# Where the value products of two attention stages stand in TensorE's queue, and how independent matmuls are dealt out between them

## The reference

```python
for window, dil in DILATED_PATTERNS:      # (128, 1), (512, 4), (2048, 16)
    o, lse = band_attention(by_residue(q), by_residue(k), by_residue(v), window // dil)
    ...
w = jax.nn.softmax(jnp.stack(lses, axis=0), axis=0)
o = jnp.sum(w[..., None] * jnp.stack(outs, axis=0), axis=0)
```

```python
g = jax.nn.sigmoid(gates)...
o = g[..., 0:1] * o_cmp + g[..., 1:2] * o_s + g[..., 2:3] * o_w
```

## Time and profile before

| | us |
|---|---|
| median of 3 runs | 3198.38 (3194.66 to 3199.76) |
| the profiled execution, its own time | 3204.74 |
| its span | 3203.0 |
| TensorE busy | 3175.9 (99%) |
| VectorE, ScalarE, GpSimd busy | 1728.2 (54%), 1149.8 (36%), 1303.5 (41%) |

### The profile page before, as it was taken

How to read it: one execution, slowest core, us unless ns; L and a number is a source line. 1 busy time by engine, 2 the same in 40 slices (tenths; PEclk the granted TensorE clock), 3 DMA queues, 4 the chain that set the end, 5 groups by cost and what they waited for, 6 DMA issues and landing times.

```text
span 3203.0 us, 40631 instructions
## 1 busy us (share of the span) xinstructions
PE 3175.9 (99%) x15480; PEld 2549.3 (80%) x15480; DVE 1728.2 (54%) x2194; ACT 1149.8 (36%) x1700; POOL 1303.5 (41%) x688
## 2 busy tenths in 40 slices
PE   9999999999999999999999999999999999999999
PEld 7888886788888888887678888876888888678887
DVE  5544546554445444446764444776645556765443
ACT  4223312532223222236752222457322343753222
POOL 4777201067672777400016765030557402115600
PEclk9999999999999999999999999989999999999999
DMA  7554331155443554331124443410434342034432
GB/s 220 147 154 148 130 110 60 54 153 148 144 153 116 144 151 157 119 96 49 53 80 137 145 150 119 95 63 28 150 131 145 118 101 90 27 99 138 131 101 82
DMA packets 338612, 371.48 MB, mean 116 GB/s; under 512 B 32704, under 2 KB 287808, under 8 KB 338240
## 3 DMA queue, kind: packets, MB, share of 16 engines
q1 hardware_dynamic: 311040, 277.99, 28.1%
q0 software_dynamic: 27456, 91.94, 9.2%
HBM read 361.92 MB, written 2.18 MB: 114 GB/s over the span
## 4 chain that ended last, share of the span: by engine, by line
PE 46%; DVE 2%; ACT 2%; issue 0%; DVEq 0%; ACTq 0%
PE ps L394 19%; PE ps L779 16%; PE ps L471 2%; PE ps L685 1%; PE ps L1109 1%; PE ps L1121 1%; PE ps L1435 1%; PE ps L625 1%; PE ps L1948 1%; PE ps L566 0%; PE ps L990 0%; PE ps L1887 0%; DVE w_lo L342 0%; DVE sb_scr_lo L1412 0%; PE ps L705 0%
## 5 line engine op out<-in xcount | busy, mean ns | idle before, releaser
L338 ACT CAST w_hi<-raw 128x2048 fp32r<-128x2048 f32 x243 | 463.8, 1909 | 1139.0 <-PE ps L394 925.0
L394 PE MATMUL ps<-h_hi,w_hi 128*128 128x512 f32 x2064 | 807.3, 391 | 1.7 <-DVE w_lo L342 1.2
L394 PE MATMUL ps<-h_hi,w_lo 128*128 128x512 f32 x2064 | 804.2, 390 | 0.0
L394 PE MATMUL ps<-h_lo,w_hi 128*128 128x512 f32 x2064 | 804.1, 390 | 0.0
L342 DVE TENSOR_TENSOR w_lo<-raw,w_hi 128x2048 fp32r<-128x2048 f32 x241 | 608.5, 2525 | 248.9 <-ACT w_hi L338 248.6
L779 PE MATMUL ps<-a_hi,w_hi 128*128 128x512 f32 x1325 | 516.6, 390 | 0.4
L779 PE MATMUL ps<-a_lo,w_hi 128*128 128x512 f32 x1325 | 515.6, 389 | 0.0
L779 PE MATMUL ps<-a_hi,w_lo 128*128 128x512 f32 x1325 | 515.5, 389 | 0.0
L394 PEld LDWEIGHTS ps<-h_hi,w_hi 128*128 128x128 f32 x2064 | 388.1, 188 | 82.2 <-DVE w_lo L342 1.7
L394 PEld LDWEIGHTS ps<-h_hi,w_lo 128*128 128x128 f32 x2064 | 388.1, 188 | 81.2
L394 PEld LDWEIGHTS ps<-h_lo,w_hi 128*128 128x128 f32 x2064 | 388.2, 188 | 79.8 <-issue 0.2
(11 more groups left out here) (385 smaller groups left out, 4115.3 us busy)
## 6 DMA issues: line engine op xcount, KB each, us to landing
raw<-in_ffn_w_in SPq DMA_DIRECT2D x174, 512.0 KB, 5.0
raw<-in_w_ff SPq DMA_DIRECT2D x128, 512.0 KB, 4.3
m_in<-in_w_mod POOLq DMA_DIRECT2D x96, 512.0 KB, 4.1
raw<-in_ffn_w_out SPq DMA_DIRECT2D x88, 512.0 KB, 4.2
m_in<-in_w_ff POOLq DMA_DIRECT2D x64, 512.0 KB, 4.0
raw<-in_hyb_w_in SPq DMA_DIRECT2D x28, 512.0 KB, 4.5
raw<-in_w_in SPq DMA_DIRECT2D x28, 512.0 KB, 4.7
raw<-in_sb_w_in SPq DMA_DIRECT2D x24, 512.0 KB, 4.1
```

What stands on the lines that cost most here:

```text
L338: eng.copy(w_hi[:, e % 2], raw[:, e % 2]).then_inc(s["w_hi_done"], 1)
L394: mm = pe.matmul(ps[:, bank], wbuf[a][:, e % 2, at:at + P], hbuf[b][:, k], start=(k == 0 and n == 0), stop=(k == KC - 1 and n == 2))
```

## The change

In two places of one function, and in the numbers that steer it. Values: a unit of a group `g >= runs` gets no values at iteration i + 1; its group's four are issued one behind the other in the iteration after its last unit. `runs` is 0 in the dilated stage (all groups) and 2 in the sparse ones (all but the first two). ScalarE's copies then wait only for the values of the groups before, not of the units before. Filling: instead of a constant number a unit gets one by its place in the group, (6, 14, 14, 14) in the dilated stage and (0, 5, 5, 6) in the sparse ones. The sums stay 96, the first unit with filling stays unit 8 and unit 7. `half_unit`, after which VectorE and ScalarE order their pieces, follows from the new shares.

```diff
         def half_unit(spec, d):
-            lo, per = spec["fill"]
-            return lo + (12 * d + 11) // per
+            return next(i for i in range(4 * len(spec["pairs"])) if filled(spec, i + 1) >= 12 * (d + 1))
+
+        def fill_share(spec, i):
+            return spec["fill"][i % 4] if i >= spec["from"] else 0
+
+        def filled(spec, upto):
+            return sum(fill_share(spec, i) for i in range(upto))
+
+        def in_one_run(spec, i):
+            return i // 4 >= spec["runs"]
...
-                if lo <= i < n:
-                    advance(fill, per)
+                if 0 <= i < n:
+                    advance(fill, fill_share(spec, i))
...
-                if i >= 1:
-                    hp, br, I = att_unit(spec, i - 1)
...
+                if i >= 1 and not in_one_run(spec, i - 1):
+                    values(i - 1)
+                elif i >= 1 and i % 4 == 0:
+                    for j in range(i - 4, i):
+                        values(j)
...
-                    eng.wait_ge(s["att_o"], a)
+                    eng.wait_ge(s["att_o"], c.att + i // 4 * 4 if in_one_run(spec, i) else a)
...
-            "pairs": [(hp, 0) for hp in range(4)], ... "fill": (8, 12), "parts": 2,
+            "pairs": [(hp, 0) for hp in range(4)], ... "fill": (6, 14, 14, 14), "from": 8, "runs": 0, "parts": 2,
...
-            "pairs": [(hp, br) for hp in range(4) for br in range(2)], ... "fill": (7, 4), "parts": 4,
+            "pairs": [(hp, br) for hp in range(4) for br in range(2)], ... "fill": (0, 5, 5, 6), "from": 7, "runs": 2, "parts": 4,
```

More of the change, by code:

```diff
@@ L1080, in pe_attention, with values @@
             n = 4 * len(spec["pairs"])
-            lo, per = spec["fill"]
             fill = pe_out_half(pe, c)
+            def values(j):
+                hp, br, I = att_unit(spec, j)
+                a, ag = c.att + j, c.attg + j // 4
+                pe.wait_ge(s["att_pt"], 2 * (a + 1))
+                if I == 3:
+                    pe.wait_ge(s["att_rc"], ag)
+                for o in range(2):
+                    mm = pe.matmul(ps[qk_rows(o), o_bank(ag), I * P:], spec["v"](br, 2 * hp + o, I),
+                                   p_T(a, o)[:, 4 * I * P:(3 * I + 4) * P], start=(I == 3), stop=(I == 0),
+                                   skip_group_check=True)
+                mm.then_inc(s["att_o"], 1)
             for i in range(-1, n + 1):
@@ L1378, in hybrid_stack_kernel @@
         dil_spec = {
-            "pairs": [(hp, 0) for hp in range(4)], "y": 16, "mask": "mask_dil", "gate": None, "layer": None, "fill": (8, 12), "parts": 2,
+            "pairs": [(hp, 0) for hp in range(4)], "y": 16, "mask": "mask_dil", "gate": None, "layer": None, "fill": (6, 14, 14, 14), "from": 8, "runs": 0, "parts": 2,
             "q": lambda h: act[qk_rows(h), DIL_AT[h // 2]],
@@ L1385, in hybrid_stack_kernel @@
         nsa_spec = {
-            "pairs": [(hp, br) for hp in range(4) for br in range(2)], "y": 4, "mask": "mask_causal", "layer": 0, "fill": (7, 4), "parts": 4,
+            "pairs": [(hp, br) for hp in range(4) for br in range(2)], "y": 4, "mask": "mask_causal", "layer": 0, "fill": (0, 5, 5, 6), "from": 7, "runs": 2, "parts": 4,
             "gate": lambda hp, br: gates[:, :, :].rearrange("p i (h b) -> p i h b", b=3)[:, :, 2 * hp:2 * hp + 2, br + 1],
```

## The result

The changed kernel takes 3217.76 us (median of 6 runs, 3212.56 to 3221.12), the kernel before in the same session 3199.07 (6 runs, 3194.66 to 3203.01): a ratio of 1.0056, 95% interval 1.0045 to 1.0067. It is slower, by 18.7 us.

What follows compares the result with a forecast made beforehand. The prediction took TensorE and the order of its queue as the bound. Two sparse layers 16.2 plus dilated stage 8.5 minus runs 2.4 gave 22.3 us slower: 3227 for the profiled execution, 3220 for the median, range 3204 to 3234.

Steps and rivals of the forecast that it cites:

- What bounds the stages: Both attention kinds: TensorE sets the time, busy 74.54 of 75 us (dilated) and 101.53 of 107 (first sparse).
- Values in one run: All three stages: 0.15 us saved a group, bounds 0 and 0.48; 16 runs save 2.4 us, between 0 and 7.7.
- sign for "wrong": Values blocks in a run spaced by columns alone (0.21 us per 128), no wait at reciprocals' turn, or period under 12.2.
- No filling in a group's first unit: Sparse stages: TensorE waits 1.3 us for VectorE at the reciprocals' turn in four units; such waits sum to 7.7 a layer.
- A layer: Each sparse stage: net 8.1 us slower before the saving of values in one run, bounds 5 and 10.
- The dilated stage: Filling waits for VectorE's additions to xT in units 10 to 15, together 6.8 us; net 8.5, 7.9 with runs' saving.
- the rival that I had given 0.13: Dilated waits of 2.3 and 2.2 us lower TensorE's clock, each drop costing 3 us: 3226; chance 0.13.
- the two smaller terms: Dilated stage: runs save 0.6 us; values leaving the first two groups cost 1.7, between zero and 3.5.
- A dear switch: Each moved values block saves 0.16 us plus 0.1 on the step ahead, 12.5 in all: +12, 3210; chance 0.18.
- Faster: Sparse stages: reciprocals slip before VectorE's maxima, the 1.3 us wait vanishes, kernel some 10 us faster, 3188; chance 0.06.

Runs made afterwards that it cites:

- the run with shares 0, 5, 6, 5: Changed kernel with three values blocks ahead of the reciprocals' turn and sparse filling 0, 5, 6, 5; dilated filling even, runs in last two groups: 3193.35 us.
- the turn later: Changed kernel with the sparse stages' turn of the reciprocals issued behind the next scores and the run's first block: 3215.89 us.
- even filling: Changed kernel with 12 filling matmuls in every unit of the dilated stage, values still in one run: 3206.87 us, dilated stage 68.25 us.
- filling alone: Changed kernel with values unit by unit as before the change, filling uneven as in the changed kernel: 3207.27 us, ratio 1.0022.

## Why the prediction was right, point by point

It said 3220 and slower; 3217.76 was measured. By its own steps:

**What bounds the stages: right.** The order of TensorE's queue does, and all of the time lies in the three stages.

**Values in one run: the mechanism right, the size wrong by three.** I took 0.15 us a run, from bounds of 0 and 0.48; 0.47 was measured (2.77 against 2.30), the upper bound. The reason that I gave for the low value, that each block still waits for its own semaphore and loads its own weights, is not borne out: when the run comes these waits have most likely been met, and the rows show the blocks closing up (starts 0.27, 0.43 and 0.64 us apart for one, two and three times 128 columns). The Trainium skill's rule (TensorEngine Tiling (Array Packing), section Key Properties), that a change of mode drains TensorE, is what the trace agrees with: three changes into the full-width form fell away per run, and 0.16 us with each. No run separates a drain from whatever else such a change costs. Scores lose a little too where values no longer follow (0.92 instead of 1.01 us for 512 columns, 0.47 instead of 0.56 for 256), which the prediction had kept at their cost. The prediction's sign for "wrong", blocks spaced by little more than their columns, came true.

**No filling in a group's first unit: the wait right, its cause half told.** 1.3 us expected at the turn of the reciprocals, 1.24 listed and 1.43 by spacing; unit 24, for which I had 2.0, waited no longer than the others, for VectorE had time to do the split beforehand; at unit 8 it was 0.3 listed and 0.55 by spacing, 0.5 expected. By spacing that is 5 x 1.43 + 0.55 = 7.7 us a layer, just the sum worked out: four waits a little longer and one shorter. For the third unit of a group I had 0.1 and for unit 22 0.9; the rows have about 0.2 (by spacing, against the run with shares 0, 5, 6, 5) and 0.74. The period came out at 13.0 (13.3 expected). What failed is the picture of the turn as all that hangs there: the next scores wait for the same maxima, and would be free only 0.4 us earlier. It made no difference to the sum, but a remedy built on it (the turn later) gained 0.3 us a layer instead of the 4 to 6 expected of it.

**A layer: +7.2 expected after the saving, +4.6 measured.** The 2.6 are the runs (6 x 0.32 = 1.9) and, for the rest, the shorter steps of the scores (0.09 in eleven places, about 1.0), less some small terms. The waits are no part of it, as said.

**The dilated stage: the waits right, 7.9 expected, 10.4 measured.** Four waits of 2.3, 1.0, 1.2 and 2.2 us were worked out; the trace has 2.16, 0.76, 0.98 and 1.88, 5.8 together (6.5 by spacing), and each at the place named. The step that failed is the clock, which the sum put at nothing: the rival that I had given 0.13 came true here, twice. In three other executions with the same filling and the same waits of 5.8 us only one of the two dips came, and the stage took 76.3 to 76.4 us instead of 77.9 (77.8 in a fourth, which had both): 1.5 us for a dip, half of what I had worked out, as the low level lasted some 3 us and not 6. That is a comparison of executions, not an experiment of its own; but the sum closes. Against even filling (68.25 us) the stage is 9.7 longer: 6.5 of waits and about 3.2 of clock, by the spacing of the slow matmuls. Of the two smaller terms the runs saved 1.9 instead of 0.6, and the first two groups cost 2.35 instead of 1.7 (68.25 - 66.84 = 1.41, and the 2 x 0.47 that runs save there).

**The total: near by errors that partly cancel.** The sparse layers came out 5.3 us under the sum, the dilated stage 2.5 over it. That the total lay as near as 3 us is in part luck: the saving of the runs was three times what I took, and the clock, left out of the sum, gave some of it back.

**The rivals.** A dear switch: true in size for the runs (7.5 us), true only in part for the step ahead of them (0.09 and not in every place), and the sum stayed near the forecast because the clock came on top. Faster: fell; nothing in the rows hides the chain of VectorE. That the run of values itself costs, a rival of the experiments: ruled out by filling alone, which costs 7.5 us without any run.

## What to carry to other kernels

Filling on an engine with an ordered queue isn't a sum to be kept but a distance: measure for each wait what time the other engine needs from the instruction that feeds it (2.1 to 2.5 us here, from the 512 column scores to their maxima and reciprocal, and 1.3 more where VectorE had other pieces ahead), and keep that much of any work between the two. When values or filling are moved, look at what they covered where they were, and when a wait has been moved away, look for the one that was hidden behind it. For filling that alternates between two banks what counts is in which unit a block ends and where the other engine takes it out, not how even the shares are.

## What the runs showed of the hardware

Taking a block of half-width matmuls out of its place between full-width ones saved about 0.16 us each time. Pauses of TensorE of 2.2 and 1.9 us were followed by a granted clock of 0.50 for about 3 us each (0.71 and 0.76 in the rows above, which take in more than the dip); the kernel before showed the lower level after a stretch in which TensorE was busy 1.64 of 4 us. With pauses of up to 1.4 us (filling alone) it stayed at 1.00. The dips don't follow from the pauses alone: of five executions with these two pauses the first was followed by a dip in three and the second in four. And in the kernel before the clock also fell where TensorE had no pause over 0.5 us, at 2084.9 us, behind 2.4 us of small matmuls (2 to 64 columns), to 0.50 until 2091.7; the changed kernel has the same small matmuls at 2092.3 and stayed at 1.00. So single executions differ by some microseconds in code that is the same.
